# Gathering the tokens of four expert groups in one pass, or group 0's first and the rest behind two expert units

## The reference, cut to what matters

```python
lg = h @ w_rg + b_rg                      # 4 groups
g_idx = argmax(lg)                        # each token goes to one group
le_g = (h @ w_re + b_re)[group g_idx]     # its 8 experts
w_k = softmax(top2(le_g)) * softmax(lg)[g_idx]
for e in range(32):
    a = silu(h @ w_gate[e]) * (h @ w_up[e])          # 1024 -> 256
    out += comb[..., e:e+1] * (a @ w_down[e])        # 256 -> 1024
return x + gate2 * out
```

## Time and profile before

| | |
|---|---|
| median of 3 runs | 1877.88 us (1874.67 to 1884.23) |
| the profiled execution | 1885.67 us, its span 1884.0 us |
| TensorE busy, share of the span | 1785.5 us, 95% |
| VectorE | 1373.1 us, 73% |
| ScalarE | 957.4 us, 51% |
| mean granted TensorE clock | 0.97 |
| HBM read | 435.36 MB, 232 GB/s over the span |

### The profile page before, as it was taken

The page is one execution under the profiler, slowest core; times in us unless marked ns, Lnnn a source line. Parts: engine busy times, 40 slices in busy tenths (PEclk is TensorE's granted clock), DMA queues, the critical chain, the costliest instruction groups (busy, mean ns, idle before and its releaser), DMA issues.

```text
span 1884.0 us, 24972 instructions
## 1 busy us (share of the span) xinstructions
PE 1785.5 (95%) x8677; PEld 1443.0 (77%) x8693; DVE 1373.1 (73%) x2091; ACT 957.4 (51%) x1433; POOL 47.0 (2%) x92
## 2 busy tenths in 40 slices
PE   5999999999999999999999999999899897999996
PEld 3788787877788878887878777887787766888875
DVE  6878675856876578777657678776776477998985
ACT  3444453664544454444436554444444546777773
POOL 0000000000000000000000000000000000000000
PEclk8999998999999999999979999999899998999998
DMA  8988651234576658884513348986563433999992
GB/s 366 362 333 302 255 203 63 93 120 170 202 288 245 247 216 322 310 325 174 191 48 110 118 150 298 350 304 231 188 246 108 183 134 138 375 350 363 359 346 98
DMA packets 61499, 437.45 MB, mean 232 GB/s; under 512 B 6768, under 2 KB 7280, under 8 KB 9200
## 3 DMA queue, kind: packets, MB, share of 16 engines
q1 hardware_dynamic: 47200, 339.27, 48.1%
q0 software_dynamic: 12672, 92.28, 13.2%
q10 hardware_dynamic: 1552, 4.89, 0.7%
HBM read 435.36 MB, written 1.05 MB: 232 GB/s over the span
## 4 chain that ended last, share of the span: by engine, by line
PE 83%; DVE 11%; ACT 4%; issue 1%; DMA 1%; ACTq 0%; SPq 0%; DVEq 0%; POOLq 0%
PE bank L1717 24%; PE bank L1718 24%; PE bank L1719 24%; DVE w_lo L933 3%; PE bank L1940 2%; DVE ada_w L957 1%; ACT w_hi L504 1%; PE bank L1958 1%; PE bank L1799 1%; DMA ada_w<-ada_pairs 1%; PE bank L1920 1%; PE bank L1707 1%; DVE arena L1032 1%; DVE w_lo L940 1%; DVE arena L1232 1%
## 5 line engine op out<-in xcount | busy, mean ns | idle before, releaser
L933 DVE TENSOR_TENSOR w_lo<-raw,w_hi 128x1024 fp32r<-128x1024 f32 x426 | 501.5, 1220 | 223.5 <-ACT w_hi L504 222.9
L504 ACT ACTIVATE w_hi<-raw 128x1024 fp32r<-128x1024 f32 x426 | 426.2, 1052 | 363.5 <-PE bank L1719 359.6
L1717 PE MATMUL bank<-w_hi,uT_hi 128*128 128x512 f32 (+3 forms) x1424 | 558.4, 392 | 19.5 <-DVE uT_lo L1251 11.9
L1718 PE MATMUL bank<-w_lo,uT_hi 128*128 128x512 f32 (+3 forms) x1424 | 544.2, 382 | 0.0
L1719 PE MATMUL bank<-w_hi,uT_lo 128*128 128x512 f32 (+3 forms) x1424 | 543.7, 382 | 0.0
L1717 PEld LDWEIGHTS bank<-w_hi,uT_hi 128*128 128x128 f32 x1424 | 271.6, 191 | 78.7 <-DVE uT_lo L1251 12.9
L1719 PEld LDWEIGHTS bank<-w_hi,uT_lo 128*128 128x128 f32 x1424 | 270.9, 190 | 52.1
L1717 PE MATMUL bank<-w_hi,r_arena 128*128 128x512 f32 (+1 forms) x744 | 301.9, 406 | 8.1 <-DVE r_arena L1634 4.9
L1718 PEld LDWEIGHTS bank<-w_lo,uT_hi 128*128 128x128 f32 x1424 | 271.5, 191 | 48.7 <-issue 1.4
L1718 PE MATMUL bank<-w_lo,r_arena 128*128 128x512 f32 (+1 forms) x744 | 298.6, 401 | 0.0
L1719 PE MATMUL bank<-w_hi,r_arena 128*128 128x512 f32 (+1 forms) x744 | 295.7, 397 | 0.0
(11 more groups left out here) (324 smaller groups left out, 1474.8 us busy)
## 6 DMA issues: line engine op xcount, KB each, us to landing
raw<-weight_stream SPq DMA_DIRECT2D x216, 1024.0 KB, 4.9
ada_w<-ada_pairs POOLq DMA_DIRECT2D x88, 1024.0 KB, 5.2
raw<-expert_blocks SPq DMA_DIRECT2D x48, 1024.0 KB, 4.9
ada_w<-expert_blocks SPq DMA_DIRECT2D x32, 1024.0 KB, 4.8
cmpw<-expert_blocks SPq DMA_DIRECT2D x16, 1024.0 KB, 4.9
arena<-ada_pairs SPq DMA_DIRECT2D x5, 1024.0 KB, 13.9
ada_w<-ada_pairs SPq DMA_DIRECT2D x3, 1024.0 KB, 13.3
cmpw<-compress_w ACTq DMA_DIRECT2D x2, 1024.0 KB, 8.1
```

Source lines behind the costliest of these rows:

```text
L504: act.activation(w_hi[:, b], v, ACT.Copy).then_inc(hi_done, 1)
L933: V.tensor_tensor(w_lo[:, b], v, f32(w_hi[:, b]), ALU.subtract).then_inc(split_done, 1)
L1717: pe.matmul(dst, xh, w_hi[:, off:off + n], start=first, stop=False, skip_group_check=True)
L1718: pe.matmul(dst, xh, w_lo[:, off:off + n], start=False, stop=False, skip_group_check=True)
```

## The change

The gather is done in two phases.

- `gather_first`: group 0 alone, 32 products of 128 columns, four chunks to a bank (banks 0 and 1), with two signals. ScalarE evacuates chunks 0 to 3 (four instructions of 128 columns), VectorE chunks 4 to 7.
- `gather_rest`: groups 1 to 3, 32 products of 384 columns, in two halves: chunks 0 to 3 behind unit 0's gate and up products, after a wait for the picks of groups 1 to 3; chunks 4 to 7 behind unit 0's down products. Their evacuations (one of 384 columns each, the even chunks on ScalarE, the odd ones on VectorE) stand between units, and the split of groups 1 and 2 moves one unit later.
- VectorE writes group 0's picks first, and those of the others only after ranks and softmax; it splits block 1 of unit 0 after group 0's low parts and no longer ahead of the logits, and ranks the experts after that.
- TensorE turns the picks in group 1, where it then waits for ScalarE's copies; those stand in ScalarE's list behind group 0's `sparse_out`.

The diff, with the parts of the fifth pass left out:

```diff
@@ -343,7 +343,7 @@
             return used[off // BLK], HYB_U0 + m + 2
 
         HYB_SET_BANKS = [(bank[0], bank[1]), (bank[2], bank[7]), (bank[2], bank[3]), (bank[2], bank[3])]
-        GATHER_BANKS = (0, 1, 2, 3, 7, 5, 6, 4)
+        REST_BANKS = (2, 3, 7, 0, 2, 3, 7, 5)
 
 
 
@@ -838,17 +838,26 @@
             act.activation(e_exp[:, :, :], e_exp[:, :, :], ACT.Exp).then_inc(exp_out, 1)
 
 
-            def gathered(n, tiles):
-
-                for j in range(4):
-                    act.wait_ge(us_psum, n * KD + 2 * j + 1)
-                    act.activation(usf[:, 0:tiles, 2 * j], bank[GATHER_BANKS[2 * j]][:, 0:tiles * P].rearrange("p (i s) -> p i s", i=tiles),
-                                   ACT.Identity, scale=modf[:, 8 + 2 * j:9 + 2 * j], bias=modf[:, 2 * j:2 * j + 1]).then_inc(usf_done_a, 1)
-
-            def gathered_hi(n, i):
+            def gathered_first(n):
+
+                act.wait_ge(us_psum, n * (2 + KD) + 1)
+                for k in range(4):
+                    e = act.activation(usf[:, 0, k], bank[0][:, k * P:(k + 1) * P], ACT.Identity, scale=modf[:, 8 + k:9 + k], bias=modf[:, k:k + 1])
+                e.then_inc(usf_done_a, 1)
                 for h in range(2):
-                    act.wait_ge(usf_done_a, n * 4 + 2 * h + 2)
-                    act.wait_ge(usf_done_v, n * 4 + 2 * h + 2)
+                    act.wait_ge((usf_done_a, usf_done_v)[h], n * 5 + 1)
+                    act.activation(us_hi[0][:, 4 * h:4 * h + 4], usf[:, 0, 4 * h:4 * h + 4], ACT.Copy).then_inc(us_hi_done, 1)
+
+            def gathered_rest(ks):
+                for k in ks:
+                    act.wait_ge(us_psum, 3 + k)
+                    act.activation(usf[:, 1:, k], bank[REST_BANKS[k]][:, 0:3 * P].rearrange("p (i s) -> p i s", i=3),
+                                   ACT.Identity, scale=modf[:, 8 + k:9 + k], bias=modf[:, k:k + 1]).then_inc(usf_done_a, 1)
+
+            def gathered_hi(i):
+                for h in range(2):
+                    act.wait_ge(usf_done_a, 5)
+                    act.wait_ge(usf_done_v, 5)
                     act.activation(us_hi[i][:, 4 * h:4 * h + 4], usf[:, i, 4 * h:4 * h + 4], ACT.Copy).then_inc(us_hi_done, 1)
 
             def picks_out(n, tiles):
@@ -885,7 +894,13 @@
                 if not first:
                     sparse_out(n - 1)
                 beside()
-                with act.Fori(0, halves - 1) as i:
+                if n == 0:
+                    sparse_unit(half, 1)
+                    gathered_rest((4, 6))
+                    gathered_hi(1)
+                    gathered_hi(2)
+                    sparse_unit(half + 1, 0)
+                with act.Fori(int(n == 0), halves - 1) as i:
                     sparse_unit(i + half, 1)
                     sparse_unit(i + (half + 1), 0)
                 sparse_unit(half + halves - 1, 1, last=last)
@@ -894,22 +909,19 @@
                     sparse_out(n)
 
             def later_tiles():
-                gathered_hi(0, 1)
-                gathered_hi(0, 2)
                 picks_out(0, EXPERT_GROUPS)
-
-            gathered(0, EXPERT_GROUPS)
-            gathered_hi(0, 0)
-
-            beside = [later_tiles, lambda: gathered_hi(0, 3), lambda: None, lambda: None]
+                gathered_hi(3)
+
+            gathered_first(0)
+
+            beside = [lambda: gathered_rest((0, 2)), later_tiles, lambda: None, lambda: None]
             for n in range(EXPERT_GROUPS):
                 expert_group(n, beside[n], n == 0, n == EXPERT_GROUPS - 1)
...
@@ -1550,11 +1562,16 @@
                   lambda: norm_tile(q6 + 2, 0), more=False)
             norm(q6 + 2, n6 + 1, (1,))
 
-            def gathered(n, tiles):
-                for j in range(4):
-                    k = 2 * j + 1
-                    dve.wait_ge(us_psum, n * KD + k + 1)
-                    V.tensor_scalar(usf[:, 0:tiles, k], bank[GATHER_BANKS[k]][:, 0:tiles * P].rearrange("p (i s) -> p i s", i=tiles),
+            def gathered_first(n):
+                dve.wait_ge(us_psum, n * (2 + KD) + 2)
+                for k in range(4, KD):
+                    e = V.tensor_scalar(usf[:, 0, k], bank[1][:, (k - 4) * P:(k - 3) * P], modf[:, 8 + k:9 + k], modf[:, k:k + 1], ALU.mult, ALU.add)
+                e.then_inc(usf_done_v, 1)
+
+            def gathered_rest(ks):
+                for k in ks:
+                    dve.wait_ge(us_psum, 3 + k)
+                    V.tensor_scalar(usf[:, 1:, k], bank[REST_BANKS[k]][:, 0:3 * P].rearrange("p (i s) -> p i s", i=3),
                                     modf[:, 8 + k:9 + k], modf[:, k:k + 1], ALU.mult, ALU.add).then_inc(usf_done_v, 1)
 
             hi_groups = [0]
@@ -1569,7 +1586,7 @@
             for t in range(T):
                 dve.wait_ge(xn_hi_done, t + 1)
                 V.tensor_tensor(xn_lo[:, t], xn[:, t], f32(xn_hi[:, t]), ALU.subtract).then_inc(xn_ready, 1)
-            expert_split(0, 0, (0, 1), IN_LINE)
+            expert_split(0, 0, (0,), IN_LINE)
 
             dve.wait_ge(r_psum, 1)
             link(V.tensor_copy(logits[:, :, :], GU[1][:, 128:256].rearrange("p (t c) -> p t c", t=T)[:, :, 0:36]))
@@ -1601,17 +1618,22 @@
             dve.wait_ge(count_psum, 1)
             V.tensor_copy(g_total, GU[1][:, 0:4])
             link(V.tensor_tensor(g_cum[:, :, :], GU[1][:, 4:12].rearrange("p (t g) -> p t g", t=T), g_sel[:, :, :], ALU.mult))
-            for g in range(EXPERT_GROUPS):
-                for t in range(T):
-                    e = V.tensor_scalar(pick[:, t, g], place_iota, g_cum[:, t, g:g + 1], None, ALU.is_equal)
-            e.then_inc(pick_ready, 1)
+
+            def picked(groups):
+                for g in groups:
+                    for t in range(T):
+                        e = V.tensor_scalar(pick[:, t, g], place_iota, g_cum[:, t, g:g + 1], None, ALU.is_equal)
+                e.then_inc(pick_ready, 1)
+
+            picked((0,))
 
             link(V.tensor_reduce(le_g[:, :, :], le_m.rearrange("p t g e -> p t e g"), AX.X, ALU.add))
             link(V.tensor_reduce(e_max, le_g[:, :, :], AX.X, ALU.max))
             V.tensor_tensor(e_exp[:, :, :], le_g[:, :, :], e_max.unsqueeze(2).to_broadcast([P, T, 8]), ALU.subtract).then_inc(exp_in, 1)
+            gathered_first(0)
+            gathered_lo(0)
+            expert_split(0, 0, (1,), IN_LINE)
             ranks(le_g, 8, e_gt, e_eq, tie8, e_rank)
-            gathered(0, EXPERT_GROUPS)
-            gathered_lo(0)
             link(V.tensor_scalar(e_rank[:, :, :], e_rank[:, :, :], 2.0, None, ALU.is_lt))
             dve.wait_ge(exp_out, 2)
             V.tensor_reduce(g_sum, g_exp[:, :, :], AX.X, ALU.add)
@@ -1622,6 +1644,7 @@
             link(V.tensor_tensor(e_sum, e_sum, p_sel, ALU.mult))
             V.tensor_tensor(e_w[:, :, :], e_exp[:, :, :], e_sum.unsqueeze(2).to_broadcast([P, T, 8]), ALU.mult).then_inc(ew_ready, 1)
             dve.wait_ge(ew_ready, 1)
+            picked((1, 2, 3))
 
             link(V.tensor_scalar(g_over, g_total, float(P), None, ALU.is_gt))
             V.tensor_reduce(over[:, 1:2], g_over, AX.X, ALU.add)
@@ -1655,7 +1678,13 @@
                 if not first:
                     sparse_out(n - 1)
                 beside()
-                with dve.Fori(0, halves - 1) as e:
+                if n == 0:
+                    sparse_unit(half, 1, i, 1)
+                    gathered_rest((5, 7))
+                    gathered_lo(1)
+                    gathered_lo(2)
+                    sparse_unit(half + 1, 0, i, 2)
+                with dve.Fori(int(n == 0), halves - 1) as e:
                     sparse_unit(e + half, 1, i, e * 2 + 1)
                     sparse_unit(e + (half + 1), 0, i, e * 2 + 2)
                 sparse_unit(half + halves - 1, 1, i, PER_GROUP - 1, last=last)
@@ -1663,17 +1692,13 @@
                     sparse_h_split(MOE_F0 + (n + 1) * PER_GROUP - 1)
                     sparse_out(n)
 
-            def later_tiles():
-                gathered_lo(1)
-                gathered_lo(2)
-
             def sparse_out(n):
                 for h in range(2):
                     dve.wait_ge(ys_hi_done, 2 * n + h + 1)
                     V.tensor_tensor(y_lo[:, h * 512:(h + 1) * 512], ACC[h][:, :], f32(y_hi[:, h * 512:(h + 1) * 512]),
                                     ALU.subtract).then_inc(ys_ready, 1)
 
-            beside = [later_tiles, lambda: gathered_lo(3), lambda: None, lambda: None]
+            beside = [lambda: gathered_rest((1, 3)), lambda: gathered_lo(3), lambda: None, lambda: None]
             for n in range(EXPERT_GROUPS):
                 expert_group(n, n, beside[n], n == 0, n == EXPERT_GROUPS - 1)
             x_update(n6 + 1, (spread_done, 1), SPREAD)
...
@@ -2252,15 +2277,25 @@
             pe.matmul(GU[1][:, 8:12], ones, g_sel[:, 0], start=True, stop=False, skip_group_check=True)
             pe.matmul(GU[1][:, 8:12], tri[:, 0:P], g_sel[:, 1], start=False, stop=True, skip_group_check=True).then_inc(count_psum, 1)
 
-            def gather(tiles):
-
```

(42 more changed lines are left out.)

13 lines of the change are left out of this document (6 added, 7 removed).

## The result

The changed kernel takes 1886.76 us (median of 21 runs, 1878.17 to 1894.16), the kernel before 1878.36 us beside it (21 runs): a ratio of 1.0045, interval 1.003 to 1.006. It is a little slower, by 8.4 us, and by less than the 0.5% that was called the bound; the interval reaches from 5.6 to 11.3 us. The forecast was +8.3 and 1886.

What follows compares the result with a forecast made beforehand. The expert stage was taken as bound by TensorE, with VectorE and the DMA close behind. Terms 2.3 + 4.2 + 1.8 gave +8.3 us, 1886 us against the median 1877.88; range 1878 to 1894.

Steps and rivals of the forecast that it cites:

- The sum: Whole kernel: 2.3 us late by unit 3, 4.2 at group 1's start, 1.8 of slow clock behind it, together +8.3 us.
- The routing and the start: Before the first unit: logits taken 1.35 us earlier, two picks instead of eight 1.25, short gather 6.8, first unit 4.6 earlier.
- The bounds: Short gather: a 128-column product at the full clock costs from 0.111 us (8-column pace) to 0.139 us (96-row float32 pace).
- The products behind S': Unit 0: TensorE ends 24 products at 5.7 us, waits 1.6 for the later picks; 4.4 us lost at its hidden rows.
- S': Start of the first unit's first product in the changed kernel, forecast at 1573.8 us, 4.6 us ahead of before.
- The two VectorE waits of 0.6 and 0.7 us: TensorE waits for VectorE at unit 0's down products (S'+18.7 to S'+19.3) and at later turned rows (S'+30.8 to S'+31.5).
- the slower rival: Slower by more than 9.4 us: clock drop at group 1 3.6, another in unit 0 1.1, +11.2 us; chance 0.35.
- Group 1: At group 1's start TensorE turns the picks, 1.1 us, then stands 3.1 for ScalarE's copies: 4.2 us lost.
- The clock behind that wait: Behind group 1's wait the clock falls to 1.2 GHz for the first dense products: 1.8 us, bounds 0 and 3.6.
- The first phase is no shorter: Rival at the short gather: loads set its pace, so only 2.6 us come of the start; counted in the slower rival.
- The covered variant: Clock rises early in the short gather and does not drop at group 1: +4.6 us; counted as within 0.5%.
- Faster: Neither wait costs and the rest of the gather fills TensorE's old waits: -2.0 us, 1876; faster by over 0.5%, chance 0.04.

Runs made afterwards that it cites:

- two_and_two: The changed kernel with the gather cut at the middle, groups 0 and 1 first, groups 2 and 3 behind; 1.0008 of the kernel before.
- wait_at_spread: The changed kernel with TensorE's wait for the copied picks moved to just ahead of group 1's spread; 1.0022 of the kernel before.

## Why the prediction was right, point by point

**The sum.** +8.3 against 8.4 measured. The milestones give 3.4 for group 0 (2.3 forecast), 4.2 for group 1 (4.2), and a clock that fell behind the wait in four of five profiled kernels at 1.6 us (1.8, taken as certain). That is some 9 us, which the interval of the ratio (5.6 to 11.3 us) holds. Group 0 is the term that was mis-sized, by 1.1. That the sum meets the median within 0.1 is luck: group 0 was too cheap, the clock too dear, and the median itself is not known to better than about 3 us.

**The routing and the start** were right: the logits at once, the gather at 5.25 instead of 7.80 (2.55, forecast 2.60), 0.215 us a product, the first unit 4.3 us earlier (4.6). The evacuations of 128 columns were 0.34 us each and not 0.3. The bounds were right too: at the full level a narrow product costs 0.112, the lower one.

**The products behind S'.** Here one step failed in its reason: "TensorE is through with the first unit's 24 products at 5.7 and waits for the picks, 1.6 us". TensorE did not wait. I had let the clock rise by the end of the short gather; it stayed at 0.50 for some 4 us of the first unit, the 24 products took 7.5 us instead of 5.7, and the picks were there. The price, 4.6 us against the forecast 4.4 at unit 0's rows, is the same, since the slow products took just the time of the wait. That the two came out alike is luck. (The sum had also slipped by 0.1: 7.2 less 5.7 is 1.5. Nothing hangs on it.) The wait is real: 0.99 us in two_and_two, where the clock is up.

**Unit 1 and unit 2.** The two VectorE waits of 0.6 and 0.7 us did not show either. In the profiled execution the clock fell once in unit 1, behind the weights' gather and its wait, and TensorE came no earlier than VectorE. I had this fall in the slower rival, at 1.1 us net. That is the microsecond by which group 0 is dearer than the sum. In wait_at_spread the clock did not fall there: unit 1's rows come 11.9 us behind unit 0's instead of 13.5, and 0.3 of the 1.5 is lost again by unit 2's. Its unit 2 is 2.6 us behind the kernel before, near the forecast 2.3.

**Group 1** was right in mechanism and size: 3.15 us of standing (3.1), ended by the picks' copies, with ScalarE's block split and y ahead of them; and two experiments, one that takes it away and one that adds it alone, show it worth its full length.

**The clock behind that wait** was argued from a row that was read too simply. In the kernel before, the level did not fall behind the idle 3.11 us but inside it, 1.3 us behind the start of the turn, as two windows of before show:

```profile
1559.90:1560.90 1.00, 0.02 (x1) 0.00 (x0) 1.00 (x2) 0.96 (x1) 0.00 (x0) 1.00 0.55 66
1561.00:1563.00 2.00, 0.00 (x0) 0.00 (x0) 1.83 (x12) 0.00 (x0) 0.00 (x0) 0.50 0.93 389
```

Ahead of it stood 1.45 us of idle, the turn, and 1.0 us of idle. So the row did not show that 3.1 us are what it takes, and in the profiled execution of the change the fall that was forecast did not come. The size, 1.6 us where it came, was near the 1.8.

**The signs.** The products of 0.21 us, the place of the first unit, the wait of 3 us on the picks' copies and a full TensorE from unit 2 on came. The 1.6 us of idle ahead of the first 384-column product did not, nor, in the profiled execution, the clock of 0.50 behind group 1's wait.

**The rivals.** Slower by over 9.4 us did not come; its parts, the two falls of the clock, are real, and each costs 1.6 us or less. "The first phase is no shorter" fell: 6.9 us against 9.4, and 3.6 against 7.5 at the full level. The covered variant asked for an early rise of the clock and none of its falls at group 1: the second half came in the profiled execution, the first did not. "Faster" asked that neither wait costs, and the 3.15 us at group 1 do.

**Why so little comes of a gather that waits for a quarter of the work.** The split of the gather moves 5.6 us of products behind the first unit, but does not remove them: both phases load all 32 weights anew. At the full level the two phases take 3.6 + 5.6 = 9.2 us against 7.5 undivided. In the change, what the early start wins is spent by unit 0's rows.
